# Stick-breaking and retention of the even mixer as four unrolled rounds, with the input projection spread through them

## What is computed

```python
def even_mixer(hn, w_in, q_gain, k_gain, ret_gain, w_out):
    sb_q, sb_k, sb_v, r_q, r_k, r_v, r_g = split(hn @ w_in)      # 7 x 512 columns
    # 8 heads of 64: z = q k^T / 8, keys strictly before the query
    #   w = exp(log_sigmoid(z) - sum over later keys of softplus(z));  out_a = w v
    out_a = stick_breaking_attention(rms_norm(sb_q), rms_norm(sb_k), sb_v)
    # 4 heads of 128: causal scores times a decay gamma^(i-j), rope on q and k
    ret = retention_chunkwise(rope(r_q), rope(r_k), r_v, log_gamma)
    out_b = rms_norm(ret, ret_gain) * silu(r_g)
    return concatenate([out_a, out_b]) @ w_out
```

## Time and profile before

| | us |
|---|---|
| median of 3 runs | 2252.96 (2244.27 to 2254.03) |
| the profiled execution, own time | 2254.68 |
| its span | 2252.9 |
| PE busy | 2057.1 (91%) |
| DVE busy | 1153.6 (51%) |
| ACT busy | 700.3 (31%) |
| POOL busy | 798.5 (35%) |

### The profile page before, as it was taken

One profiled execution on the slowest core, in us unless ns is written; L12 is line 12 of the kernel. 1 busy time (PEld: TensorE's weight loads), 2 busy tenths in 40 slices (PEclk: granted clock), 3 DMA queues, 4 the chain that ended last, 5 costly groups with the idle time before them and its releaser, 6 DMA issues.

```text
span 2252.9 us, 28840 instructions
## 1 busy us (share of the span) xinstructions
PE 2057.1 (91%) x10008; PEld 1597.1 (71%) x10008; DVE 1153.6 (51%) x2007; ACT 700.3 (31%) x1289; POOL 798.5 (35%) x412
## 2 busy tenths in 40 slices
PE   5999998878999969899878999999899888999999
PEld 4877776656777748566536888888587666888887
DVE  5628997777984351444444555522422435555511
ACT  2125655025531131444412333300223323333200
POOL 1442221326854424211103444444242123444444
PEclk9999999889999979999969999999899899999999
DMA  3621110312112222111102232233222112332332
GB/s 113 177 94 35 33 39 20 94 48 62 61 38 93 90 77 96 43 47 37 38 0 75 87 101 93 95 101 112 68 91 67 38 48 76 97 99 93 99 126 75
DMA packets 55143, 167.48 MB, mean 74 GB/s; under 512 B 8064, under 2 KB 16128, under 8 KB 54800
## 3 DMA queue, kind: packets, MB, share of 16 engines
q1 hardware_dynamic: 47760, 155.22, 21.4%
q10 hardware_dynamic: 7296, 11.08, 1.7%
HBM read 157.88 MB, written 2.10 MB: 71 GB/s over the span
## 4 chain that ended last, share of the span: by engine, by line
PE 71%; DVE 13%; issue 8%; ACT 3%; POOL 2%; SPq 2%; ACTq 1%; DMA 1%; DVEq 0%; POOLq 0%
PE bank L164 14%; PE bank L166 14%; PE bank L165 14%; PE bank L494 2%; PE bank L495 2%; PE bank L496 2%; SPq L141 2%; PE bank L269 2%; PE bank L270 2%; POOL wlo L149 1%; PE bank L271 1%; DVE prob L1247 1%; DVE ssb L1234 1%; PE bank L2094 1%; PE bank L2092 1%
## 5 line engine op out<-in xcount | busy, mean ns | idle before, releaser
L149 POOL TENSOR_TENSOR wlo<-raw,whi 128x1024 fp32r<-128x1024 f32 x260 | 625.2, 2405 | 1205.7 <-DVE whi L155 1205.7
L155 DVE CAST whi<-raw 128x1024 fp32r<-128x1024 f32 x288 | 200.6, 697 | 671.1 <-PE bank L166 515.3
L164 PE MATMUL bank<-xh,whi 128*128 128x512 f32 x928 | 364.5, 393 | 11.7 <-POOL wlo L149 8.5
L165 PE MATMUL bank<-xl,whi 128*128 128x512 f32 x928 | 362.9, 391 | 0.0
L166 PE MATMUL bank<-xh,wlo 128*128 128x512 f32 x928 | 362.6, 391 | 0.0
L164 PEld LDWEIGHTS bank<-xh,whi 128*128 128x128 f32 x928 | 175.4, 189 | 50.8 <-POOL wlo L149 10.2
L166 PEld LDWEIGHTS bank<-xh,wlo 128*128 128x128 f32 x928 | 175.4, 189 | 37.0
L165 PEld LDWEIGHTS bank<-xl,whi 128*128 128x128 f32 x928 | 175.5, 189 | 36.4
L164 PE MATMUL bank<-ghi,whi 128*128 128x512 f32 x352 | 136.9, 389 | 0.0
L165 PE MATMUL bank<-glo,whi 128*128 128x512 f32 x352 | 136.9, 389 | 0.0
L166 PE MATMUL bank<-ghi,wlo 128*128 128x512 f32 x352 | 136.9, 389 | 0.0
(11 more groups left out here) (359 smaller groups left out, 3881.7 us busy)
## 6 DMA issues: line engine op xcount, KB each, us to landing
raw<-in_weights_dram SPq DMA_DIRECT2D x288, 512.0 KB, 3.5
h<-in_x_dram SPq DMA_DIRECT2D x1, 2048.0 KB, 8.3
sz<-su SPq DMA_DIRECT2D x128, 16.0 KB, 1.8
out_dram<-h ACTq DMA_DIRECT2D x4, 512.0 KB, 2.8
etab<-in_even_tables_dram ACTq DMA_DIRECT2D x1, 1730.0 KB, 6.5
x_kh<-kvc_h ACTq DMA_DIRECT2D x2, 256.0 KB, 3.9
x_kl<-kvc_l ACTq DMA_DIRECT2D x2, 256.0 KB, 5.4
x_vh<-kvc_h ACTq DMA_DIRECT2D x2, 256.0 KB, 8.3
```

The lines of the kernel that those rows point to most:

```text
L149: nc.gpsimd.tensor_tensor(wlo[:, s % 2, :], raw[:, s, :], whi[:, s % 2, :].bitcast(F32), ALU.subtract).then_inc(w_lo, 1)
L155: nc.vector.tensor_copy(whi[:, t_of_4 % 2, :], raw[:, t_of_4, :]).then_inc(w_hi, 1)
L164: nc.tensor.matmul(to, w_h, pe_h, start=first and k == 0, stop=False)
L165: nc.tensor.matmul(to, w_h, pe_l, start=False, stop=False)
```

## The change

- The two hardware loops are gone. Four rounds are written out; a round is one pair of stick-breaking heads, then one retention head.
- The weights are reordered so that the projection tiles come as q, k, v, rq, rk, rv, rg for round 0, then for round 1, and so on. PE makes only the first four (q, k, v, rq) ahead of the rounds. The other 24 tiles (96 quarters) are spread: round 0 has 24 quarters, rounds 1 and 2 have 28 each, round 3 has 16. The retention of round 3 has 14 chunks of the first two output tiles beside it in their place.
- The two heads of a pair are interleaved (unit u: head u % 2, key block 3 - u // 2), logits have three banks in place of two, and the weights of a pair lie in packed buffers for both heads.
- The sum over later key blocks is kept as a running sum: DVE adds the later block's softplus to the next block's (`running_sum`, 4 in a round), and PE needs one matmul with ones where it had one per later block.
- Norm squares come straight from the PSUM bank; the copies of v go away; rg gets its Silu as it is taken from the bank.
- PE waits for `e_loaded` at the start of `pe_even`, ahead of the first projection tile; before it waited behind the twelfth.
- The output projection has its own function: chunk 7 of tiles 0 and 1 comes after the last retention head, then tiles 2 to 7.

```diff
         def pe_even(pe):
-            products_from_norm(pe, "even_in", ORDER[N_MIX0])
-            products_feature_major(pe, "even_in", 4, 4)
-            products_token_major(pe, "even_in", 8, 4)
-            pe.wait_ge(tv_taken, TV0["even_in"] + 4)
             pe.wait_ge(e_loaded, 48)
-            with pe.Fori(0, 4) as i:
...
+            products_from_norm(pe, "even_in", ORDER[N_MIX0], between=lambda j: pe_head_squares(pe, 0) if j == 2 else None)
+            for i in range(4):
+                pe_stick(pe, i, beside)
+                pe_retention(pe, i, beside if i < 3 else lambda n: pe_even_out_beside(pe, n))
+        def pe_stick(pe, i, beside):
+            between = iter((2, 2, 1, 2, 1, 2, 1, 2, 3) if i else (1, 2, 1, 1, 1, 2, 1, 1, 2))
...
+            def later_sums(p):
+                for hd in range(2):
+                    u, jb = 2 * p + hd, 3 - p
+                    pe.wait_ge(e_sp, 8 * i + u + 1)
...
+                    if p >= 2:
+                        pe.wait_ge(e_run, 4 * i + 2 * (p - 2) + hd + 1)
+                    mm = nc.tensor.matmul(to[:, 0:S - jb * P], later_key, packed(esp, hd, jb), start=True, stop=jb == 3)
+                    if jb < 3:
+                        mm = nc.tensor.matmul(to[:, P:S - jb * P], ones, packed(esp, hd, jb + 1), start=False, stop=True)
# order on PE: beside, turn v, logits(0), beside, logits(1), beside, later_sums(0), beside, logits(2), beside,
# later_sums(1), beside, logits(3), beside, later_sums(2), beside, later_sums(3), turn rv, beside, outputs
+        def pe_retention(pe, i, beside):
# swap x2, beside(3), scores x4, beside(4), outputs x4, beside(2), ones x1, squares of the next pair x2, beside(3)
# order on DVE in dve_stick:
+            soft(0)
+            soft(1)
+            split("A")
+            soft(2)
+            soft(3)
+            split("B")
+            log_weight(0)
+            log_weight(1)
+            mask_weight(0)
+            mask_weight(1)
+            soft(4)
+            soft(5)
+            split("C")
+            for u in (2, 3):
+                log_weight(u)
+                running_sum(u)
+            split("D")
...
+            soft(6)
+            soft(7)
+            for u in (4, 5):
+                log_weight(u)
+                running_sum(u)
+            def running_sum(u):
+                hd, jb, w = unit(u)
+                nc.vector.tensor_tensor(packed(esp, hd, jb, P), packed(esp, hd, jb, P), packed(esp, hd, jb + 1),
+                                        ALU.add).then_inc(e_run, 1)
+        def pe_even_out(pe, n):
+            pe.wait_ge(r_lo, 4)
+            for m in range(KC):
+                if m >= 2:
+                    pe.wait_ge(w_lo, T0["even_out"] + m + 1)
+                    pe.wait_ge(acc_free[m % 2], (O0["even_out"] + m) // 2 + 1)
+                for k in range(KC) if m >= 2 else (KC - 1,):
+                    mm = pe_even_out_chunk(pe, m, k)
+                mm.then_inc(tile_done, 1)
```

More of the change, by code:

```diff
@@ L272, in products_from_norm @@
                 mm.then_inc(tile_done, 1)
-                if j == 0 and between is not None:
-                    between()
+                if between is not None:
+                    between(j)
         def freed(o, i=0, per=0):
@@ L443, in build @@
         e_ol = sem("e_ol")
-        STEPS = [(hd, jb) for hd in range(2) for jb in (3, 2, 1, 0)]
         def tile_of(x, i):
@@ new lines, in unit, with pe_head_squares, pe_turn_token_major @@
+        def unit(u):
+            return u % 2, 3 - u // 2, S - (3 - u // 2) * P
+        def pe_head_squares(pe, i):
+            for j in range(2):
+                pe.wait_ge(e_sqr, 2 * i + j + 1)
+                nc.tensor.matmul(bank[2 + j][:], bdiag, et[:, 2 + j, :], start=True, stop=True).then_inc(e_ms, 1)
+        def pe_turn_token_major(pe, name, i, to):
+            even_taken(pe, name, i)
+            for b in range(4):
+                mm = nc.tensor.transpose(to[:, b * P:(b + 1) * P], sq[:, ("v", "rv").index(name), b * P:(b + 1) * P], ident)
+            mm.then_inc(tv_turned, 1)
@@ L582, in pe_even, with beside @@
-            pe_retention(pe)
+            products_from_norm(pe, "even_in", ORDER[N_MIX0], between=lambda j: pe_head_squares(pe, 0) if j == 2 else None)
+            parts = iter(range(16, 28 * 4))
+            def beside(n):
+                for _ in range(n):
+                    product_beside(pe, "even_in", 0, 0, 4, next(parts))
+            for i in range(4):
+                pe_stick(pe, i, beside)
+                pe_retention(pe, i, beside if i < 3 else lambda n: pe_even_out_beside(pe, n))
@@ L584, in act_even, with act_head_rstd @@
+        def act_head_rstd(act, i):
+            for j in range(2):
+                act.wait_ge(e_ms, 2 * i + j + 1)
+                nc.scalar.activation(er[:, j, :], bank[2 + j][:], ACT.Ln, bias=(e64eps, epsc)[j],
+                                     scale=(64.0, 1.0)[j]).then_inc(e_ln, 1)
+            for j in range(2):
+                act.wait_ge(e_ln, 2 * i + j + 1)
+                nc.scalar.activation(er[:, j, :], er[:, j, :], ACT.Exp, scale=-0.5).then_inc(e_r, 1)
         def act_even(act):
@@ L593, in act_even @@
[L593 to L640, removed]
@@ L2323, in _ @@
                     pe_even(pe)
[L2324 to L2326 removed]
+                    pe_even_out(pe, after)
                 if name == "odd":
```

464 lines of the change are left out of this document (284 added, 180 removed).

## The result

The changed kernel takes 2186.55 us in the median (2186.16 to 2186.98, 4 runs); beside it the kernel before took 2250.23 (2244.27 to 2254.03, 4 runs). The ratio is 0.9718, with a 95% interval of 0.9695 to 0.9741: 2.8% faster, 64 us by the medians. Forecast were 2210 and a range of 2192 to 2232. The direction was right and the gain half as large again as forecast.

The account below looks back on a forecast made before the run. PE's work plus its waits was taken to bound the kernel. Start 873.7, rounds 65.5, 69, 69 and 55.3, then tail and output projection gave 1179.1 against 1222.9, 43.8 us less: about 2210 us, range 2192 to 2232.

Parts of the forecast that it names:

- What bounds the kernel: Even mixer: PE's work plus its waits bound it; the retention loop had PE busy 42 of 65.2 us, without projection beside it.
- The wait that moved: Start of the projection: PE waits for the tables until 844.7 in place of beginning at 829.36, costing 13.7 us.
- The sum: Start, rounds, tail and output projection added up: end at 1179.1 in place of 1222.9, a gain of 43.8 us.
- A middle round, walked through: Rounds 1 and 2: PE's work walked beside the ACT and DVE chain, giving a period of 69 us.
- the term for PE's work: Middle round: quarters 38.1, columns 24.2, turns 1.3 and visits 4.4 us, together 68.0.
- The bounds: Limits for a round: 64.6 us with nothing lost to visits, 79 with every low part holding DVE up.
- the change does more than I think: Rival for the whole kernel: rounds at 65 us and a tail hidden better, 2190 us; chance 0.05.
- The wait at the fourth later sums: Middle round, later_sums(3): PE waits some 0.3 us for DVE's running sums 4 and 5.
- the chain sets the rounds: Rival: port meetings and in-order lists make PE wait at later_sums; rounds 76 to 79 us, 2238 to 2250; chance 0.11.
- The shared port: Rounds: DVE operations contend with POOL's low parts; three meetings a round matter, the running sum behind split C taking 2.3 us.
- The tail: After the last outputs: 6.5 us to the low part's end, then 1.3 and 3.2 us until output tile 2.
- nothing behind it is changed: Behind the output projection: no change, so the mixer's gain of 43.8 us is the whole gain.

Follow-up runs that it names:

- the two experiments: Kernel before with PE waiting for the tables ahead of its first projection tile: 2263.48 us; changed kernel with that wait behind the third projection tile: 2173.95 us.
- logits apart: Changed kernel with three projection matmuls between the two logits of a pair and three behind them: 2191.50 us.
- The split put behind the sums: Changed kernel with the split of rk (rounds 1 to 3) behind the first two running sums in DVE's order: 2179.33 us.
- outputs apart: Changed kernel with all four output matmuls of head 0 before all four of head 1, in place of one of each in turn: 2190.56 us.
- the tail filled: Changed kernel with four of round 3's fourteen output chunks moved from beside the decay to behind the last matmul with ones: 2179.95 us.
- the version with no running sums and the other two edits: Changed kernel with PE's tables wait late, four round 3 output chunks moved behind the last ones matmul, and PE's ones matmuls replacing running sums: 2168.60 us.

## Why the prediction was wrong, point by point

**What bounds the kernel; the retention chain hidden under the projection: right.** The stretch of 65 us with PE busy for 42 is gone, and with it 22.8 us in which PE stood; no run here undoes this alone. The two heads side by side are worth about as much against the kernel before: there a pair's logits and outputs took 5.75 and 4.60 us in the timeline of PE, here they take 2.97 and 2.30, which is 5.1 us a round and 20 in all. PE now stands for 0.31 us in a whole retention half (0.69 in the last), and quarters never waited for `w_lo`.

**The wait that moved: right,** 13.7 us predicted, 13.4 and 13 measured in the two experiments. The low clock behind the start lasted 4.4 us and not 6, which is 1 us.

**The sum failed in "A middle round, walked through", in the term for PE's work.** Its parts against round 1 of the trace (starts differenced, in us):

| part of a middle round | predicted | measured |
|---|---|---|
| logits, 2560 columns | 4.3 | 3.0 |
| outputs, 2560 columns | 4.3 | 2.3 |
| later sums, 4096 columns | 6.9 | 6.6 |
| swap, scores, outputs, ones, squares | 8.65 | 7.9 |
| turns | 1.3 | 0.9 |
| 28 quarters and 11 visits | 42.5 | 40.95 |
| waits | 0.8 | 2.2 |
| together | 68.8 | 63.8 |

3.4 of the 5 us are the two heads side by side. I read a price per column from the earlier trace rows, where every matmul of a pair stood alone or next to one of the same head, and put it on an order of instructions where they don't. I had listed the interleaving as a change of order and costed it at nothing. The outputs and logits apart show that this is its worth: 1.56 and 2.9 us a round, 11.6 us by the medians when both are undone. The second is more than the 1.3 us in the table, because the price of 1.69 ns a column was also too low for logits alone: one head of 512 columns took 1.05 us in the kernel before, which is 2.05 ns a column. Two errors of opposite sign met in that term. The visits were priced 1.5 us a round too high, the small f32 matmuls of the retention 0.7, the later sums and turns together 0.7; against that stands 1.4 us more of waiting than walked.

The bounds failed with the price. The floor that the prediction gave a round, 64.6 us with nothing lost to visits, already holds 8.6 us for logits and outputs where 5.3 were taken, so the measured 63.8 lay below it. The rival "the change does more than I think", at a chance of 0.05, came nearest with 2190, but for rounds at 65 us and a better tail, and not for this mechanism.

The Trainium skill (TensorEngine Tiling (Array Packing), Key Properties) states that tiles of the array operate independently, and that different tiles can run their weight loads and matmuls in parallel. The measured pairs agree: 1.06 us for two heads, 1.05 for one. I did not weigh this against the change, and it bore on it.

**The wait at the fourth later sums: right in place, 0.3 us predicted, 1.87 measured.** In round 1 PE came there 22.9 us behind the first logits and not 26.0, of which 1.4 us are the packed logits and 1.4 the cheaper visits. The running sum that it needs let it go on at 24.8 us and not at 26.3; the blocked one took 2.35 us, and I had put 2.3. So the chain is what a middle round is bound by at that point, and the rival "the chain sets the rounds" had its mechanism there: 7.5 us, and not 28 or more, with some low clock behind it.

**The shared port: right,** one meeting in three mattered. The split put behind the sums shows it.

**The tail: right** in both gaps (4.34 us for the low part after one of 0.69, 1.93 for `w_lo`).

**The part called "nothing behind it is changed"** is right of the code; why this pair of profiles differs by 4.6 us there stays open, beyond the higher granted clock over most of it. The kernel before varied by 10 us from run to run.

## What to carry to other kernels

Price a matmul with its neighbour: two small ones that use different halves of the array's rows or columns cost as much as one here when they were adjacent, and only the differences of starts show it, since each one's recorded duration stays the same. When work is moved off the critical engine, ask what the engine that takes it over has queued behind it: the same sum cost 5 us in one order and gained 10 in another, the clock included. And give every wait the latest place that its first user allows; one wait was 13 us.

## What the runs showed that I had not expected

- Two logits matmuls of 64 contraction rows each, f32, 512 columns: 1.06 us together, 1.05 alone. Two output matmuls of 64 columns each, into the same PSUM bank but other partitions, likewise: 2.30 us for both heads interleaved, 2.30 for one head alone in the kernel before, 3.86 when all of one head comes before all of the other.
- Waits of nearly the same length did not have the same effect on the clock. The wait of 1.87 us ahead of the fourth later sums left the full clock in rounds 1 and 2; in round 3 of the same execution one of 1.89 us was followed by the low one, 1.42 us for matmuls that take 0.94. With the outputs apart it was the other way round: low behind the waits of 1.90 us in rounds 1 and 2, full behind that of 1.87 in round 3. The first two rows are of the changed kernel, the third is of outputs apart:

```profile
1084.96 1.62 PE L589 MATMUL bank<-esp,etab 128*128 128x512 f32 x2 [1.89 <-DVE esp L765]
1086.38 1.48 PE L591 MATMUL bank<-esp,tables 128*128 128x384 f32 x2
```
```profile
957.57 1.91 PE L589 MATMUL bank<-esp,etab 128*128 128x512 f32 x2 [1.90 <-DVE esp L765]
```

- At the end of the mixer gaps of 4.34 and 1.93 us brought the low clock until 1129.7 in the changed kernel, and gaps of 1.61 and 2.52 us none with the tail filled. The gaps alone do not decide it: with outputs apart (first two rows below) the full clock was back right behind the same gap of 1.93 us, and in the version with no running sums and the other two edits (last two rows) the gap of 2.52 us was followed by the low one. No run here tells what decides between them.

```profile
1130.08 0.50 PE L883 MATMUL bank<-eo_h,whi 128*128 128x512 f32 x1 [1.93 <-POOL wlo L149]
1130.42 0.40 PE L884 MATMUL bank<-eo_l,whi 128*128 128x512 f32 x1
```
```profile
1103.08 0.65 PE L883 MATMUL bank<-eo_h,whi 128*128 128x512 f32 x1 [2.52 <-POOL wlo L149]
1103.52 0.63 PE L884 MATMUL bank<-eo_l,whi 128*128 128x512 f32 x1
```
